# Moving weight splits, ada blocks, decay rows and ada columns in the first third of a two-block transformer kernel on one Trainium2 core

## What is computed

```python
def ada_modulation(c, w, b):
    mod = jax.nn.silu(c) @ w + b
    shift, scale, gate = jnp.split(mod, 3, axis=-1)
    return shift[:, None], scale[:, None], gate[:, None]

def gated_deltanet_layer(h, in_w, conv_w, A_log, dt_bias, onorm_g, out_w):
    proj = h @ in_w
    qkv = jax.nn.silu(causal_depthwise_conv(proj[..., :3 * A_WIDTH], conv_w))
    z = proj[..., 3 * A_WIDTH:4 * A_WIDTH]
    b = proj[..., 4 * A_WIDTH:4 * A_WIDTH + A_HEADS]
    a = proj[..., 4 * A_WIDTH + A_HEADS:]
    ...
    beta = jax.nn.sigmoid(b)
    g = -jnp.exp(A_log) * jax.nn.softplus(a + dt_bias)
    o = chunk_gated_delta_rule(q, k, v, g, beta)
    o = rmsnorm(o, onorm_g) * jax.nn.silu(z)
    return o.reshape(Bn, T, A_WIDTH) @ out_w

for l in range(DEPTH):
    shift, scale, gate = ada_modulation(c, ada_w[l], ada_b[l])
    h = rmsnorm(x, norm_g[l]) * (1.0 + scale) + shift
    out = gated_deltanet_layer(h, ...) if l == 0 else nsa_layer(h, ...)
    x = x + gate * out
```

## Time and profile before

| | us |
|---|---|
| median of 3 runs | 1109.83 |
| lowest and highest | 1108.64 and 1111.14 |
| the profiled execution | 1113.65 |
| its span, first to last instruction | 1111.9 |
| PE busy | 1042.9 (94%) |
| DVE busy | 697.3 (63%) |
| ACT busy | 593.0 (53%) |
| POOL busy | 113.9 (10%) |

### The profile page before, as it was taken

How to read it: one execution, slowest core, us unless ns; L and a number is a source line. 1 busy time by engine, 2 the same in 40 slices (tenths; PEclk the granted TensorE clock), 3 DMA queues, 4 the chain that set the end, 5 groups by cost and what they waited for, 6 DMA issues and landing times. The chain is left out here.

```text
span 1111.9 us, 17013 instructions
## 1 busy us (share of the span) xinstructions
PE 1042.9 (94%) x7074; PEld 934.0 (84%) x7074; DVE 697.3 (63%) x1007; ACT 593.0 (53%) x889; POOL 113.9 (10%) x111
## 2 busy tenths in 40 slices
PE   2599989799999999999999999999999989999997
PEld 2499978698899788878888789988989969889996
DVE  5779775666675665668656555555556786554454
ACT  3355566564564545537466664444345986444443
POOL 1100018362120001123000010000000200000000
PEclk9799999999899999999999999999999999999999
DMA  9766435524377633214632346555554445555540
GB/s 322 238 188 180 133 107 189 178 89 133 78 218 265 209 127 120 76 39 153 205 136 80 111 152 214 177 181 193 185 188 130 155 132 184 194 181 187 183 171 38
DMA packets 120428, 178.42 MB, mean 160 GB/s; under 512 B 5188, under 2 KB 80098, under 8 KB 120352
## 3 DMA queue, kind: packets, MB, share of 16 engines
q1 hardware_dynamic: 118816, 172.40, 48.0%
q0 software_dynamic: 1120, 2.97, 0.9%
q10 hardware_dynamic: 416, 1.97, 0.5%
HBM read 176.27 MB, written 1.05 MB: 159 GB/s over the span
## 5 line engine op out<-in xcount | busy, mean ns | idle before, releaser
L1350 DVE TENSOR_TENSOR sb_w_lo<-sb_raw,sb_w_hi 128x2048 fp32r<-128x2048 f32 (+2 forms) x141 | 319.8, 2268 | 218.2 <-ACT sb_w_hi L709 217.8
L709 ACT ACTIVATE sb_w_hi<-sb_raw 128x2048 fp32r<-128x2048 f32 (+2 forms) x141 | 265.9, 1888 | 141.7 <-PE G L2154 112.8
L2152 PE MATMUL X<-sb_hT_hi,sb_w_hi 128*128 128x256 f32 x960 | 273.1, 285 | 4.2 <-DVE sb_hT_lo L1683 2.1
L2153 PE MATMUL X<-sb_hT_lo,sb_w_hi 128*128 128x256 f32 x960 | 271.1, 282 | 0.0
L2154 PE MATMUL X<-sb_hT_hi,sb_w_lo 128*128 128x256 f32 x960 | 271.0, 282 | 0.0
L2152 PEld LDWEIGHTS X<-sb_hT_hi,sb_w_hi 128*128 128x128 f32 x960 | 183.1, 191 | 6.8 <-issue 3.2
L2153 PEld LDWEIGHTS X<-sb_hT_lo,sb_w_hi 128*128 128x128 f32 x960 | 183.1, 191 | 0.6
L2154 PEld LDWEIGHTS X<-sb_hT_hi,sb_w_lo 128*128 128x128 f32 x960 | 183.2, 191 | 0.0
L2152 PE MATMUL G<-sb_w_hi,sb_uT_hi 128*128 128x512 f32 x304 | 121.3, 399 | 4.8 <-DVE sb_uT_lo L2092 4.8
L2153 PE MATMUL G<-sb_w_lo,sb_uT_hi 128*128 128x512 f32 x304 | 120.7, 397 | 0.0
L2154 PE MATMUL G<-sb_w_hi,sb_uT_lo 128*128 128x512 f32 x304 | 120.7, 397 | 0.0
(11 more groups left out here) (448 smaller groups left out, 1736.6 us busy)
## 6 DMA issues: line engine op xcount, KB each, us to landing
sb_raw<-in_mlp_w SPq DMA_DIRECT2D x64, 1024.0 KB, 5.2
sb_raw<-in_ada_w SPq DMA_DIRECT2D x24, 1024.0 KB, 5.3
sb_raw<-in_a_in_w SPq DMA_DIRECT2D x16, 1024.0 KB, 5.8
sb_raw<-in_b_in_w SPq DMA_DIRECT2D x16, 1024.0 KB, 5.6
sb_raw<-in_sb_w_qkv SPq DMA_DIRECT2D x12, 1024.0 KB, 5.2
sb_raw<-in_rg_w_in SPq DMA_DIRECT2D x8, 1024.0 KB, 5.3
sb_raw<-in_a_out_w SPq DMA_DIRECT2D x4, 1024.0 KB, 5.1
sb_raw<-in_b_out_w SPq DMA_DIRECT2D x4, 1024.0 KB, 5.1
```

The source lines that it names most:

```text
L709: nc.scalar.activation(w_hi[s][:, 0:nk * w], raw[b % RAW_SLOTS][:, 0:nk * w], ACT.Copy).then_inc(S["w_hi"], 1)
L1350: nc.vector.tensor_tensor(w_lo[s][:, 0:nk * w], raw[b % RAW_SLOTS][:, 0:nk * w], w_hi[s][:, 0:nk * w].bitcast(F32), ALU.subtract).then_inc ...
L2152: dt32(out, lh, rh, start=first, stop=False, skip_group_check=shared)
L2153: dt32(out, lh, rl, start=False, stop=False, skip_group_check=shared)
```

## The change

The first modulation, the first split blocks and the a_ba product change places; the decay's steps, the strict rows of the second head group, four splits and the second ada columns move; two kinds of rows become transposes. In full:

1. ACT computes `silu(c)` first and issues x and then the constants after it. It also takes over the multiply with the norm for the first layer.
2. DVE does one sum, the rel_bias pieces, and then seven sums.
3. The split of a_ba goes to small tiles of its own (`few_w`), so block 2's split doesn't wait for a_ba's product. ACT's and DVE's order is: two transposed groups, block 1's split, the other two groups, block 2's split.
4. PE makes, for each of the eight slices of the first half block, a_ba's product and then the block's (`first_block`). The transposes of a_ba's result stand after block 1, the decay's steps on DVE and ACT in block 1 of the loop, the cumulated decay after block 3, its copy after block 4, and beta after the loop.
5. `strict_rows` of group 2 go into banks T0 and G3 at the end of group 1's levels, their arguments and exponentials into its tail. `strict_rows` and `decay_rows` are transposes of a spread column.
6. In both groups the first early split stands ahead of level 0, and the second one is made by DVE in two halves, one in level 0 and one in level 1.
7. `ada_columns` of the second layer is made in two halves of 8 columns, with a tile of the out product between them.

The core of the diff:

```diff
@@ opening, ACT
-            act.dma_start(consts[:, :], I["consts"]).then_inc(S["consts_in"], 16)
-            act.dma_start(xres[:, :, :], I["x"].rearrange("b (m p) d -> p (b m) d", p=P)).then_inc(S["x_in"], 16)
             act.wait_ge(S["params_in"], 16)
             nc.scalar.activation(csil[:, :], param("c"), ACT.Silu).then_inc(S["csil"], 1)
+            act.dma_start(xres[:, :, :], I["x"].rearrange("b (m p) d -> p (b m) d", p=P)).then_inc(S["x_in"], 16)
+            act.dma_start(consts[:, :], I["consts"]).then_inc(S["consts_in"], 16)
             act.wait_ge(S["consts_in"], 16)
             norm_stats(0)
+            for m in range(MT):
+                act.wait_ge(S["rstd"], m + 1)
+                nc.scalar.activation(xn[:, m, :], xres[:, m, :], ACT.Copy, scale=rstd[:, m:m + 1]).then_inc(S["xn_ready"], 1)
...
             split_hi(0)
+            transposed_hi("h0", shifted=0, groups=range(2))
             split_hi(1)
-
-            transposed_hi("h0", shifted=0)
-
+            transposed_hi("h0", shifted=0, groups=range(2, 4))
+
+            split_hi(2)
             few_copy("a_ba", 2 * AH)
-            split_hi(2)
-            log_exp_tables()
-            act.wait_ge(S["ba_min"], 1)
...
@@ loop over the a_qkv blocks, ACT
                 split_hi(m + 2)
+                if f == 1:
+                    decay_exps()
                 if f >= 1:
                     conv_silu(f - 1)
@@ head groups, ACT
             for hg in range(2):
-                for m in range(MT):
-                    act.wait_ge(S["dec_arg"], 4 * hg + m + 1)
-                    nc.scalar.activation(mt_[m][:, :, :], mt_[m][:, :, :], ACT.Exp).then_inc(S["dec"], 1)
+                if hg == 0:
+                    strict_decay(0)
+                early = m_z + 2 if hg == 0 else first_mm["a_out"]
+                split_hi(early)
                 for m in range(MT):
                     act.wait_ge(S["d1T"], turned(hg, 0, m))
                     nc.scalar.activation(dd[m][:, :, :], quad((X[0], TB[1])[m]), ACT.Copy).then_inc(S["d1"], 1)
-                    if (hg, m) == (1, 0):
-                        split_hi(first_mm["a_out"])
-                if hg == 0:
-                    split_hi(m_z + 2)
-                    split_hi(m_z + 3)
+                split_hi(early + 1)
                 z_gate(hg, 1)
...
                 if hg == 0:
+                    strict_decay(1)
                     ada_products(14)
@@ opening, DVE
-            for _i in range(3):
-                ada_sum()
+            ada_sum()
...
-            for _i in range(3):
+            for _i in range(7):
                 ada_sum()
-            norm_apply("h0")
-            for _i in range(2):
-                ada_sum()
+            split_lo(0)
             modulation(0)
-            split_lo(0)
-            shifted_lo("h0", 0)
+            shifted_lo("h0", 0, range(2))
             split_lo(1)
+            shifted_lo("h0", 0, range(2, 4))
+            split_lo(2)
@@ loop over the a_qkv blocks, DVE
                 split_lo(m + 2)
+                if f == 1:
+                    decay_first()
...
                 if f == 1:
+                    decay_last()
+                if f == 4:
                     dve.wait_ge(S["gc_done"], 1)
@@ head groups, DVE
+                early = m_z + 2 if hg == 0 else first_mm["a_out"]
+                split_lo(early)
...
-                    if l == 0:
-                        split_lo(m_z + 2 if hg == 0 else first_mm["a_out"] + 1)
+                    if l < 2:
+                        split_lo(early + 1, l)
...
-                    if l == 0:
-                        if hg == 0:
-                            split_lo(m_z + 3)
-                        else:
-                            gate_row_0(0)
+                    if l == 0 and hg == 1:
+                        gate_row_0(0)
...
                 if hg == 1:
                     y0_lo(0)
+                else:
+                    strict_args(1)
@@ PE
+            def first_block():
+
+                _, few_hi, few_lo = take()
+                pe.wait_ge(S["mod"], 1)
+                split = None
+                for c in range(2):
+                    cs = slice(c * P, (c + 1) * P)
+                    for k in range(KC):
+                        if c == 0:
+                            fresh("h0", k)
+                            ins = few_product(few_hi, few_lo, 2 * AH, k)
+                            if k == KC - 1:
+                                ins.then_inc(S["w_used"], 1)
+                        if split is None:
+                            split = take()[1:]
+                        hi, lo = split
+                        ins = passes(X[0][:, c * T:(c + 1) * T], (hi[:, k, cs], lo[:, k, cs]), hT(k), k == 0, k == KC - 1)
+                ins.then_inc(S["w_used"], 1)
...
-                        ins = dt32(quad((G[1], TB[1])[m])[:, h, :], spread(ge[:, m, 4 * hg + h:4 * hg + h + 1]), ident,
-                                   start=True, stop=True)
+                        ins = transpose(quad(STRICT_BANK[group][m])[:, h, :], spread(ge[:, m, 4 * group + h:4 * group + h + 1]), ident)
...
-                        ins = dt32(quad(X[0])[:, h, :], spread(gcs[:, m, 4 * hg + h:4 * hg + h + 1]), ident, start=True, stop=True)
+                        ins = transpose(quad(X[0])[:, h, :], spread(gcs[:, m, 4 * hg + h:4 * hg + h + 1]), ident)
...
                 else:
-                    strict_rows(0)
                     pe.wait_ge(S["zs_tile"], 2)
                     z_piece(1, 1, 0)
+                    z_piece(1, 1, 1)
                     pe.wait_ge(S["o1_sb"], 1)
-                    strict_rows(1)
-                    z_piece(1, 1, 1)
...
+                if hg == 0:
+                    for m in range(MT):
+                        strict_rows(1, m)
                 pe.wait_ge(S["inv_d"], (hg + 1) * 12)
...
+                    if (n, m) == (0, 0):
+                        ada_columns(1, 20, range(8))
                 ins.then_inc(S["w_used"], 1)
                 if n == 0:
-                    ada_columns(1, 20)
+                    ada_columns(1, 20, range(8, 16))
```

More of the change, by code:

```diff
@@ L768, in transposed_hi @@
                     act.wait_ge(S["mod"], shifted + 1)
-                for g in range(4):
+                for g in groups:
                     bank = TR_BANK[call][g]
@@ L862, in _ @@
             log_exp_tables()
+            act.wait_ge(S["ba_sp"], 1)
+            nc.scalar.activation(beta[:, :, :], basp[:, :, 0:8], ACT.Exp, scale=-1.0).then_inc(S["beta"], 1)
             act.wait_ge(S["sq_used"], 2)
@@ L1407, in transposed_lo, with shifted_lo @@
                     ins.then_inc(S["hT_lo"], 1)
-            def shifted_lo(call, layer):
-                for g in range(4):
+            def shifted_lo(call, layer, groups=range(4)):
+                for g in groups:
                     whole = tpair[g % 2][:, :, :]
@@ L1522, in spread_arg, with strict_args @@
                 ins.then_inc(S["dec_arg"], 1)
+            def strict_args(group):
+                for m in range(MT):
+                    dve.wait_ge(S["dec_rows"], 4 * group + m + 1)
+                    spread_arg(mt_[m], STRICT_BANK[group][m], m, group, "neg_strict")
             def gate_row_0(i):
@@ L2298, in _, with few_product, few_rows @@
             transposes("h0")
-            ada_columns(0, 8)
+            ada_columns(0, 8, range(16))
+            def few_product(hi, lo, n, k):
+                return passes(G[0][0:n, 0:T], (hi[:, k, :], lo[:, k, :]), hT(k), k == 0, k == KC - 1)
+            def few_rows(call, n):
+                pe.wait_ge(S["few"], 1 if call == "h0" else 2)
+                for m in range(MT):
+                    ins = transpose(G[1][:, m * n:(m + 1) * n], few[0:n, m * P:(m + 1) * P], ident[0:n, 0:n])
+                ins.then_inc(S["few_T"], 1)
             def few_columns(call, n):
@@ L2326, in key_norms @@
                 squared_norms(1, 1, 0)
-            for f in range(12):
+            for f in range(1, 12):
                 if f >= 2:
```

115 lines of the change are left out of this document (64 added, 51 removed).

## The result

| us | before | changed |
|---|---|---|
| first comparison: median (lowest to highest) | 1109.25 (1108.64 to 1111.14), 4 executions | 1094.75 (1094.51 to 1095.51), 4 executions |
| second comparison: median (lowest to highest) | 1109.50 (1108.49 to 1112.24), 9 executions | 1095.59 (1094.30 to 1097.39), 4 executions |
| the profiled execution | 1113.65 | 1094.64 |

The ratio is 0.9852 with a 95% interval of 0.9835 to 0.987 in the first comparison, and 0.9865 (0.9846 to 0.9883) in the second. The changed kernel is 14 to 15 us faster; 19.0 us were forecast, from 1109.83 to 1090.8. Between the two profiled executions lie 19.0 us, so the gain hangs on which execution of before it is measured from. A fall of the clock is, in what follows, a stretch in which the granted clock goes from 1.00 (2.4 GHz) to 0.50 (1.2 GHz).

A forecast was written before the change was run, and what follows sets the result against it. DMA was taken to bound the kernel up to 44 us, then PE. Gains of 4.1 (opening), 12.2 (head groups) and 2.7 (columns) sum to 19.0: 1113.65 to 1094.7, less 3.8 to the median: 1090.8 us, range 1086 to 1098.

The forecast's parts named there:

- Part A: The opening: earlier block landing and a new order of splits and products gain 4.1 us (0 to 6.5).
- Part B: The DeltaNet's two head groups: moved splits, transposed rows and an earlier entry to group 2 gain 12.2 us (7 to 14).
- The entry: Start of head group 2, up to its level 0: less waiting, lower clock and rows gain 5.3 us.
- the chain: DVE's three operations per half where head group 2 begins: next to be late, charged at 1.1 us.
- the clock's term: Where head group 2 begins: half of the 3.5 us at clock 0.51 is won, 1.75 us.
- Rival 3: A new wait where head group 2 begins, from DVE or ACT, costs 5.6 us: 1096.4 us; chance 0.12.
- no PE gap over 1 us: Sign expected between 190 and 225 us, around head group 2's start, together with a clock of 1.00.
- Part C: The second modulation's ada columns: halved, they keep the clock from falling, gaining 2.7 us (0 to 2.8).
- No 1: Levels 2 to 5 of both head groups: transposes make the clock fall, 44 us slower, 1135 us; chance 0.04.
- no 2: The opening wins nothing, as constants land late or DMA only reshuffles: 1095 us; chance 0.12.
- no 4: The second ada columns: the clock falls in the halves all the same, 1093.5 us; chance 0.10.
- no 5: A later stage swallows the gain, so the change doesn't do what it says: about 1108 us; chance 0.04.

The follow-up runs named there:

- the execution of 1109.43: Profiled execution, in a follow-up run, of the kernel before, unedited: 1109.43 us; that run's median was 1112.65 us of 12 executions, ratio to before 1.0004.

## Why the prediction was right and where it was wrong

- **Part A, 4.1 us.** Measured: 4.1, the lead at 79 us. Landing 42.35 (42.0 taken), start 46.64 (46.2), ACT's copy 56.94 (57.1). The price of PE's restart was 4.0 us at 0.21 instead of 0.12 us per product, so 1.8 instead of 2.4 (2.8 in the execution of 1097.39). The modulation was ready at 39.3, not 38, still under the bound of 39.5, by 0.2 us only. The experiments give 3.6 us to the order and 1.2 to the loads and sums.
- **Part B, 12.2 us.** Measured: 11.5, term by term from the leads (forecast in brackets). Group 1's split 1.07 (1.1), the four decay rows 1.8 (1.8), group 2's strict rows 0 (-0.1), level 0 of group 2 2.7 (2.6), level 1 1.7 (1.5). The entry is the miss: 4.2 instead of 5.3, since level 0 begins 11.4 us after the product at 190.05 instead of 10.2. DVE's operations between SBUF tiles took 1.67, 1.07 and 1.65 us here beside GpSimd's sum, not one of them. I charged 1.1 us for the chain; the waits are 0.61 and 1.28. The leads show what became of the clock's term: through the stretch in which before ran at half clock the lead grows from 10.3 to 11.7 us, and at the wait of 1.28 it drops to 10.5. So the missing fall gave 1.4 us, not 1.75, and DVE's chain took 1.2 of it back. Rival 3 came true with 1.1 of its 5.6 us, and without the fall of the clock. The sign "no PE gap over 1 us" between 190 and 225 therefore failed, by the wait of 1.28. And the start of level 0 of group 2, expected near 199.7 and measured at 201.43, was placed 0.9 too early by a slip: the 2.8 us for group 1 hold all four decay rows, but two of them lie in group 2, behind that point.
- **Part C, 2.7 us.** Measured: 3.2 between the profiled executions, but nothing against the other execution of before, and nothing in the traced execution with the columns together. The step that failed is the unspoken other half of "I take it that it doesn't fall": that the clock always falls without the edit. It fell in one of three traces. That it doesn't fall with the halves came out so in all eleven traces, but no run shows that the halving is the reason.
- **From the profiled execution to the median.** This is the step that failed. The sum 1113.65 - 19.0 = 1094.65 met the profiled 1094.64. That it met it to 0.01 us is luck: B was 0.7 too high, C 0.5 too low, and 0.2 us come from a place that the sum didn't have (the lead grows from 4.1 to 4.3 before group 1's level 0). Then I took off another 3.8 us because that execution stood so far above the median. But it stood there because all three falls had happened in it (1.75, 1.75 and 2.7 us by my own terms), and the sum had already counted those falls as gains. The same microseconds were taken twice. Against the execution of before without the last two falls they measured 1.6 and 3.3 us. From the execution of 1109.43, with C at nothing and B without the fall in level 1 (1.75), the same steps give 1109.43 - 4.1 - 10.45 = 1094.9 us.
- **The pieces by the medians.** Undone one at a time, against 1095.2 us, they cost 4.2 (order), 1.2 (loads and sums), 2.4 (rows), 4.6 (entry of group 2), 3.9 (splits) and nothing (columns). The sum of 16.3 us is a little more than the 14 to 15 us that they win together; medians of four to six executions that scatter by 1 to 3 us don't tell the two apart.
- **Rivals.** No 1 (clock falls in the inverse) didn't show in any trace; no 2 is excluded by both experiments on the opening; no 4 didn't show in the profiled execution; nor did no 5, since the lead stays to the end. The forecast of 1090.8 us is 4.0 below the measured 1094.75, which the range of 1086 to 1098 holds; a range of 12 us is wide enough to hide such an error. Rivals 2 and 4 name times that lie nearer (1095 and 1093.5), but 2's mechanism is excluded, and 4's end (C wins nothing) came about the other way round: the clock stayed up in two of the three traces without the halving.

## What to carry to other kernels

Ask of every term whether it occurs in each execution or only in the profiled one; a difference between that execution and the median is a clue to such terms, not a constant to subtract at the end. Where a kernel's own executions scatter by more than the term in question, profile it a second time before costing a stall of the clock. In an opening, what PE waits for last should be the smallest piece of work that lets it start; here the order across the engines was worth 3.6 us, and bytes moved earlier together with the sums 1.2.

## What the hardware showed that I had not expected

- The same wait brings the clock down in one execution and not in the next: 1.68 us with a fall and without one in two executions of the changed kernel; before level 1 of group 2, 2.76 us with a fall and 2.44 without; the 32 instructions of the ada columns with a fall in one execution (4.67 us long) and without one in two (3.63 us). In one trace waits of 0.53 and 0.97 us stood ahead of a fall. The Trainium skill (TensorE: Matmul & The Clock Gate, Part 1) describes a monitor that judges PE's activity on its own time grid; such a grid would meet a wait in a different phase each time, and the scatter agrees with that. No run here shows the monitor itself.
- The granted clock of a row and PE's pace can differ. From 46.6 to 50.6 us of the changed kernel the clock read 1.00 in one execution and, in another, 0.50, with products every 0.21 us in both:

```profile
46.60:50.60 4.00, 3.56 (x16) 3.02 (x17) 3.93 (x8) 1.68 (x1) 0.00 (x0) 0.50 0.81 203
```

- In the first of these executions the products came at 0.21 us for 4.0 us and in the second for 6.1 us before they came at 0.12, behind waits of 3.51 and 3.47 us in the first and of 3.50 and 4.11 in the second.
